# Three gate tiles of the merge fed into the chunk loop of the backward RWKV pass, and modulation blocks moved elsewhere

## The reference

```python
gates = jax.nn.sigmoid(h @ w_gate + b_gate)
acc = gates[..., :D_MODEL] * (ys[0] @ w_branch[0])
for i in range(1, N_BRANCH):
    acc = acc + gates[..., i * D_MODEL:(i + 1) * D_MODEL] * (ys[i] @ w_branch[i])
return acc @ w_o
```

## Time and profile before

| | us |
|---|---|
| median of 3 runs (lowest, highest) | 1781.99 (1780.87, 1786.96) |
| the profiled execution | 1783.33 |
| its span, first to last instruction | 1781.5 |
| PE busy | 1616.1 |
| DVE, ACT, POOL busy | 913.7, 783.3, 302.2 |
| granted PE clock, mean | 0.972 of full speed |

### The profile page before, as it was taken

The page is one execution under the profiler, slowest core; times in us unless marked ns, Lnnn a source line. Parts: engine busy times, 40 slices in busy tenths (PEclk is TensorE's granted clock), DMA queues, the critical chain, the costliest instruction groups (busy, mean ns, idle before and its releaser), DMA issues.

```text
span 1781.5 us, 35712 instructions
## 1 busy us (share of the span) xinstructions
PE 1616.1 (91%) x15480; PEld 1325.9 (74%) x15480; DVE 913.7 (51%) x1435; ACT 783.3 (44%) x1286; POOL 302.2 (17%) x241
## 2 busy tenths in 40 slices
PE   3799999977689999799999999899988789979997
PEld 1588767766566668488888886887876678979997
DVE  0444355466335433655555224655676436567754
ACT  1532355564225233634434323624765344565653
POOL 1023023512010000011112100131441110002210
PEclk9799999999899999899999999999999999989999
DMA  8742255504385212123222634734513275425554
GB/s 238 215 145 95 93 180 171 163 17 144 98 269 168 85 47 95 48 95 95 95 95 80 118 96 150 219 120 137 165 58 121 51 256 171 143 95 178 184 159 120
DMA packets 230347, 234.67 MB, mean 132 GB/s; under 512 B 5872, under 2 KB 217072, under 8 KB 230064
## 3 DMA queue, kind: packets, MB, share of 16 engines
q1 hardware_dynamic: 210560, 190.17, 34.0%
q0 software_dynamic: 15024, 35.92, 7.3%
q10 hardware_dynamic: 4608, 6.29, 1.1%
HBM read 216.63 MB, written 15.73 MB: 130 GB/s over the span
## 4 chain that ended last, share of the span: by engine, by line
PE 64%; DVE 5%; issue 5%; ACT 4%; DMA 1%; POOL 0%; ACTq 0%; DVEq 0%; POOLq 0%
PE ps L1792 15%; PE ps L1793 15%; PE ps L1794 15%; PE ps L2136 4%; PE ps L1994 2%; PE ps L1981 2%; PE ps L2033 1%; DVE wlo L1254 1%; PE ps L1830 1%; DVE X L1321 1%; ACT whi L849 1%; PE ps L1955 1%; PE ps L1815 1%; PE ps L1944 1%; DMA ring<-in_ffn_up 1%
## 5 line engine op out<-in xcount | busy, mean ns | idle before, releaser
L849 ACT ACTIVATE whi<-ring 128x1024 fp32r<-128x1024 f32 (+1 forms) x264 | 275.6, 1046 | 566.5 <-PE ps L1794 505.6
L1254 DVE TENSOR_TENSOR wlo<-ring,whi 128x1024 fp32r<-128x1024 f32 (+1 forms) x264 | 327.5, 1244 | 228.3 <-ACT whi L849 227.4
L1792 PE MATMUL ps<-H,whi 128*128 128x512 f32 (+1 forms) x656 | 220.8, 337 | 2.4 <-DVE wlo L1254 2.4
L1793 PE MATMUL ps<-H,whi 128*128 128x512 f32 (+1 forms) x656 | 220.6, 336 | 0.0
L1794 PE MATMUL ps<-H,wlo 128*128 128x512 f32 (+1 forms) x656 | 220.6, 336 | 0.0
L1792 PE MATMUL ps<-HR,whi 128*128 128x512 f32 (+1 forms) x592 | 211.6, 357 | 2.2 <-DVE wlo L1254 1.8
L1794 PE MATMUL ps<-HR,wlo 128*128 128x512 f32 (+1 forms) x592 | 207.7, 351 | 0.0
L1793 PE MATMUL ps<-HR,whi 128*128 128x512 f32 (+1 forms) x592 | 207.7, 351 | 0.0
L1792 PEld LDWEIGHTS ps<-H,whi 128*128 128x128 f32 x656 | 124.6, 190 | 16.0 <-issue 3.2
L1793 PEld LDWEIGHTS ps<-H,whi 128*128 128x128 f32 x656 | 124.6, 190 | 12.7
L1794 PEld LDWEIGHTS ps<-H,wlo 128*128 128x128 f32 x656 | 124.6, 190 | 12.7
(11 more groups left out here) (307 smaller groups left out, 3043.3 us busy)
## 6 DMA issues: line engine op xcount, KB each, us to landing
ring<-in_ada_w SPq DMA_DIRECT2D x48, 1024.0 KB, 5.8
ring<-in_ffn_up SPq DMA_DIRECT2D x44, 1024.0 KB, 5.1
ring<-in_w_gate SPq DMA_DIRECT2D x32, 1024.0 KB, 6.9
ring<-in_w_in SPq DMA_DIRECT2D x24, 1024.0 KB, 5.3
ring<-in_ffn_down SPq DMA_DIRECT2D x32, 512.0 KB, 3.8
WB<-in_w_branch POOLq DMA_DIRECT2D x8, 1024.0 KB, 7.9
ring<-in_w_o SPq DMA_DIRECT2D x8, 1024.0 KB, 5.2
ring<-in_ffn_down SPq DMA_DIRECT2D x16, 384.0 KB, 4.0
```

The costliest lines, as they stand in the source:

```text
L849: act.activation(whi[:, m % SPLIT, 0:kn, :], ring[:, SLOT[raw] % RING, 0:kn, P * half:P * half + P], ACT.Copy).then_inc(hi_done, 1)
L1254: dve.tensor_tensor(wlo[:, m % SPLIT, 0:kn, :], ring[:, SLOT[raw] % RING, 0:kn, P * half:P * half + P], whi[:, m % SPLIT, 0:kn, :].bitcast ...
L1792: pe.matmul(o[:, c0:c1], hi[:, i, :], part(0, k), start=(k == 0), stop=False)
L1793: pe.matmul(o[:, c0:c1], hi[:, i, :], part(1, k), start=False, stop=False)
```

## The change

The gate tiles (0, 2), (1, 2) and (0, 3), given as (tile, branch), are computed inside the chunk loop of the backward pass, a few matmuls at a time: 5 (layer 0) or 6 (layer 1) in each of its 14 gaps, the rest in the last. Their three splits move ahead of the loop. They use banks 5 to 7; the jobs of the backward loop share banks 0 to 4. The modulation blocks leave that loop: in layer 0 for the new point `mid` (three, between `ss` 1 and `ss` 2), with `end` of layer 0 keeping three; in layer 1 attention has seven points instead of three, the forward loop six instead of five, `mid` three. `mean` (with DVE's centring and ACT's squares) moves behind branch 2, `var` behind branch 0. `WB`'s first load goes out ahead of the wait for `y23`, and `state` moves from 112 to 168 KB to make room. The splits of `up` move from `wo` into ACT's squares of `X` and, on DVE, behind the residual. `gains` for `ffn_post` move to the end of the layer.

```diff
-READOUT = {(0, 2): "var", (0, 1): "g2"}
+READOUT = {(0, 2): "mean", (0, 0): "var", (0, 1): "g2"}
...
-CHUNK_FILL = {0: range(1, 7), 1: range(1, 6)}
+CHUNK_FILL = range(1, 7)
+GATES_AHEAD = [(0, 2), (1, 2), (0, 3)]
+GAP_PRODUCTS = {0: 5, 1: 6}
...
-        return [("chunk", l, d, c) for d in range(2) for c in CHUNK_FILL[l]]
+        return [("chunk", l, 0, c) for c in CHUNK_FILL]
...
-    before = [("att", 0, i) for i in range(0, 32, 2) if i % 8] + chunks(0)
-    after = [("end", 0, 0)] * 3 + [("att", 1, i) for i in range(0, 12, 4)] + chunks(1)
+    before = [("att", 0, i) for i in range(0, 32, 2) if i % 8] + chunks(0) + [("mid", 0, 0)] * 3 + [("end", 0, 0)] * 3
+    after = [("att", 1, i) for i in range(0, 14, 2)] + chunks(1) + [("mid", 1, 0)] * 3
...
+def chunk_gaps(l, d):
+
+    gaps, at = {}, 0
+    total = 3 * KT * len(GATES_AHEAD) if d else 0
+    order = [g for c in range(NCH) for g in (("cu", c), ("ch", c)) if g not in (("cu", 0), ("ch", NCH - 1))]
+    for n, g in enumerate(order):
+        more = total - at if n == len(order) - 1 else min(GAP_PRODUCTS[l], total - at)
+        gaps[g] = range(at, at + more)
+        at += more
+    return gaps
+
+
+def gates_done(l, d, gap):
+
+    return [("gate", l) + GATES_AHEAD[n // (3 * KT)] for n in chunk_gaps(l, d)[gap] if n % (3 * KT) == 3 * KT - 1]
 
...
+def in_first_group(name):
+
+    if name[0] in ("mean", "var", "g2"):
+        return True
+    return name[0] in ("br", "gate") and name[2] < 2 and name[2:] not in GATES_AHEAD and (name[0] == "gate" or name[3] != 3)
+
+
+def beside_gates(name, k):
+
+    if name[0] == "gate" and name[2:] in GATES_AHEAD:
+        return 5 + GATES_AHEAD.index(name[2:])
+    if name[0] in ("cu", "ch") and name[2] == 1:
+        return 4 if name[0] == "ch" else 2 * (name[3] % 2)
+    if name[0] in ("y1", "y23") and name[2] == 1:
+        return 2 * name[3]
+    return k
+
+
...
+        if g % NBANK == NBANK - 1 and in_first_group(name):
+            g += 1
+        k = beside_gates(name, g % NBANK)
...
-        state = at("state", 112, [NCH, 2, HD])
+        state = at("state", 168, [NCH, 2, HD])
...
+                    if J == 0:
+                        pool.wait_ge(mm_done, done_at(("y23", l, 1, 1)))
+                        for x in range(2):
+                            pool.wait_ge(gate_saved[x], 16 * 8 * (l + 1))
...
+                    if d == 1:
+                        act.wait_ge(kapw_done, 2 * it + 2)
+                        act.wait_ge(betaw_done, 2 * it + 2)
+                        split_until(half_no(("gate", l) + GATES_AHEAD[0]) + SPLIT)
                     for c in range(NCH):
...
+                            if (j, i) == GATES_AHEAD[0]:
+                                emptied(act, ("ch", l, 1, NCH - 2))
...
-                        split_until(min(half_no(("wo", l, j)) + 1 + SPLIT, half_no(("up", l, 0, 0)) + SPLIT))
+                        split_until(min(half_no(("wo", l, j)) + 1 + SPLIT, half_no(("up", l, 0, 0))))
...
-                split_until(half_no(("up", l, 0, 0)) + SPLIT)
                 norm_root(l, 1)
+                fill(("mid", l, 0))
                 for i in range(KT):
                     act.wait_ge(x_ready, 16 * l + i + 1)
                     square(SQB[:, i, c0:c1], X[:, i, c0:c1])
+                    if i >= 5:
+                        split_until(half_no(("up", l, 0, 0)) + i - 4)
...
+                    if d == 1:
+                        split_until(half_no(("gate", l) + GATES_AHEAD[0]) + SPLIT)
                     for p in range(2):
                         emptied(dve, ("tok", l, d, "b", p))
+                    dve.wait_ge(bonus_done, 4 * l + 2)
                     dve.memset(state[:, 0, :, :], 0.0).then_inc(state_zero, 1)
                     for p in range(2):
...
-                    if d == 1:
-                        split_until(half_no(("gate", l, 0, GATE_ORDER[0])) + SPLIT)
...
-                gains(l, (1, 2, 3))
+                fill(("mid", l, 0))
+                gains(l, (1, 2))
                 dve.wait_ge(x_back, 16 * (l + 1))
                 residual(l, 1, OB)
                 dve.wait_ge(x_ready, 16 * l + 8)
+                split_until(half_no(("up", l, 0, 0)) + SPLIT)
                 norm_apply(l, 2, X, YB, H2)
...
+            def gate_products(l, d, gap):
+
+                for n in chunk_gaps(l, d)[gap]:
+                    name = ("gate", l) + GATES_AHEAD[n // (3 * KT)]
+                    k, part = n % (3 * KT) // 3, n % 3
+                    c0, c1 = cols(l)
+                    if n % (3 * KT) == 0:
+                        if n == 0:
+                            pe.wait_ge(h_back[l], 32)
+                        ahead[name] = (job(name, JOB[name] - count[0]), next(halves(name)))
+                    o, (hi, lo) = ahead[name]
+                    last = pe.matmul(o[:, c0:c1], (hi, hi, lo)[part][:, k, :], HG[:, (0, 1, 0)[part], k, c0:c1],
+                                     start=(k == 0 and part == 0), stop=(k == KT - 1 and part == 2))
+                    if k == KT - 1 and part == 2:
+                        done(last)
+
+            ahead = {}
...
+                            gate_products(l, d, ("cu", c))
                             fill(("chunk", l, d, c), "mod")
...
+                            gate_products(l, d, ("ch", c))
                             fill(("chunk", l, d, c), "modt")
...
-                pe.wait_ge(h_back[l], 32)
                 for J in range(4):
                     for i in GATE_ORDER:
                         for j in (2 * J, 2 * J + 1) if i not in GATE_EARLY else ():
+                            if (j, i) in GATES_AHEAD:
+                                continue
...
+                        if READOUT.get((J, i)) == "mean":
+                            for p in range(2):
+                                emptied(pe, ("y23", l, 1, p))
+                                o = job(("mean", l, p))
...
                 sum_squares(l, 1, SQB)
+                fill(("mid", l, 0))
                 sum_squares(l, 2, SQB)
```

More of the change, by code:

```diff
@@ L778, in _ @@
                         .then_inc(h_back[l], 16)
-                pool.wait_ge(mm_done, done_at(("y23", l, 1, 1)))
-                for x in range(2):
-                    pool.wait_ge(gate_saved[x], 16 * 8 * (l + 1))
                 for J in range(4):
@@ L868, in norm_finish @@
                 no = 2 * l + k // 2
[L869 removed]
+                act.wait_ge(gains_ready, 3 * l + 1 + k // 2)
                 shift = 0 if k == 0 else 24
@@ L1156, in roots, with deviations @@
                            .then_inc(ln_root, 1)
-                for p in range(2):
-                    emptied(act, ("mean", l, p))
-                    act.activation(RO[:, p, c0:c1], YB[:, 6 + p, c0:c1], ACT.Square).then_inc(ln_sq, 1)
+                def deviations():
+                    for p in range(2):
+                        emptied(act, ("mean", l, p))
+                        act.activation(RO[:, p, c0:c1], YB[:, 6 + p, c0:c1], ACT.Square).then_inc(ln_sq, 1)
                 for J in range(4):
@@ L1268, in gains @@
             def gains(l, ks):
-                for n in range(24):
-                    if 0 not in ks or n < 8:
-                        emptied(dve, ("modt", l, n))
+                for n in {(0,): range(8), (1, 2): range(8, 20), (3,): range(20, 24)}[ks]:
+                    emptied(dve, ("modt", l, n))
                 for k in ks:
@@ L1688, in _ @@
                                 dve.tensor_tensor(o, o, gt, ALU.add).then_inc(gated, 1)
+                        if READOUT.get((J, i)) == "mean":
+                            centred()
                         if READOUT.get((J, i)) == "g2":
@@ L1738, in _ @@
                     emptied(dve, ("down", l, j))
+                gains(l, (3,))
                 residual(l, 3, F)
@@ L2112, in _ @@
                         done(last)
-                for p in range(2):
-                    emptied(pe, ("y23", l, 1, p))
-                    o = job(("mean", l, p))
-                    done(pe.matmul(o[:, c0:c1], K("heads"), YB[:, 6 + p, c0:c1], start=True, stop=True))
                 pe.wait_ge(ya_ready, 2 * l + 2)
@@ L2138, in _ @@
                             done(last)
-                        if READOUT.get((J, i)) == "var":
+                        if READOUT.get((J, i)) == "mean":
+                            for p in range(2):
+                                emptied(pe, ("y23", l, 1, p))
+                                o = job(("mean", l, p))
+                                done(pe.matmul(o[:, c0:c1], K("heads"), YB[:, 6 + p, c0:c1], start=True, stop=True))
+                        elif READOUT.get((J, i)) == "var":
                             for p in range(2):
```

30 lines of the change are left out of this document (14 added, 16 removed).

## The result

| | kernel before | kernel after |
|---|---|---|
| median, range of 4 runs each, us | 1784.47 (1780.87 to 1788.77) | 1806.45 (1803.06 to 1807.96) |
| profiled execution, time / span, us | 1783.33 / 1781.5 | 1806.97 / 1804.9 |
| granted TensorE clock over the span | 0.972 | 0.959 |

The ratio is 1.0121, 95% interval 1.0095 to 1.0147, that is 22 us. The prediction was 1798 (1782 to 1807), and its sum +16.1 us. In a later comparison the same kernel came out at 1.0121 again (1.0091 to 1.0150).

A forecast was written before the change was run, and what follows sets the result against it. TensorE, busy 91%, was taken as the bound, with short waits to win. Terms 0.1 + 0.8 + 4.4 + 5.8 + 4.5 + 0.5 = +16.1 us took 1783.33 to 1799.4, or 1798 on the median's scale; range 1782 to 1807.

The forecast's parts named there:

- the four places: In each layer: backward chunk loop, its tail up to the merge, norms between `wo` and `up`; second layer only: attention.
- Start of the loop: Start of the backward chunk loop: splits queued ahead delay the first `nu` product, losing 6.9 us per layer.
- The loop itself: Backward chunk loop: steps of 3.3 and 2.5 us plus slow clock lose 5.5 us (layer 0) and 1.1 (layer 1).
- To the `D` branch products: From the last `cu` to the first readout-dependent branch product: gains 12.3 us (layer 0) and 7.2 (layer 1).
- Norms: Between `wo` and `up`: late residual and splits among ACT's squares lose 4.4 us (layer 0) and 5.8 (layer 1).
- Attention and forward loop: Layer 1: four more modulation blocks in attention lose 4.5 us, one more in the forward loop 0.5.
- The feeding itself comes out even: Backward loop's start, loop and tail to the `D` branch products together: +0.1 us in layer 0, +0.8 in layer 1.
- the one in which more is late: Rival: loads competing ahead of the loop and banks holding up the merge cost 6 to 10 us more, 1806; 13%.
- The readout that keeps up: Rival: PE isn't stopped at the `D` branch products, 20 us more gained, kernel at 1778, not slower; 12%.

The follow-up runs named there:

- the early splits: Kernel after, with the fed gate tiles' three splits moved from the backward chunk loop's start into the last three levels of that pass: 1788.9 us, ratio 1.0021.
- the run with three products a gap: Kernel after plus four fixes (earlier splits, one activation table, readout earlier, additions later), three gate products a gap instead of five and six: 1762.3 us, 0.9889.
- The late additions: Kernel after, with DVE adding the `mid` blocks behind the residual and ACT copying each block's row behind a square of `X`: 1806.4 us, 1.0111.
- the two repairs: Kernel before, with one activation table for the readout's Ln and Exp and DVE's readout ahead of the second early branch's products: 1777.8 us, 0.9946.

## Why the prediction was right, and where it was off

The direction and the four places were right, and the time lies in the range, at its upper end (1806.45 of 1807); 16.1 us were forecast, 22 measured between the medians and 23.4 between the two spans that the terms below split.

1. *Start of the loop*, 6.9 us per layer: 6.5 and 6.4, by the queues described; confirmed by the early splits.
2. *The loop itself*, 5.5 and 1.1 us: 8.6 and 4.9. This is the term that was mis-sized, by 6.9 us in sum. The step was forecast as 3.3 and 2.5 us and is 3.71 and 2.81: the run with three products a gap shows 0.37 us a step that belong neither to the products nor to the recurrence, which I had not charged, over seven steps 2.6 us in each layer. The low clock costs 2.7 and 3.6 us instead of 2.0 and 1.1. Together that is a little more than what was missing. In the second execution of the same kernel layer 1 lost 3.1 us here instead of 4.9, so this term moves by some 2 us with the clock from one execution to the next.
3. *To the `D` branch products*, gain 12.3 and 7.2: from the last `cu` to there it is 33.2 and 22.6 us, a gain of 14.8 and 10.3. I had given the waits as about 6 and 11 us; they are 4.5 and 8.3. In layer 1 the first `GB` came sooner than the 6.4 us of the earlier trace rows: issued at 1475.8, used from 1480.1 on. In layer 0 ACT came to it only 6.4 us behind its issue and found it there. Of the 5.6 us more, 3.4 are lost again by the last branch product. A part of that is PE coming out of the wait slow: the eight products behind it take 5.9 us in layer 0, where they took 3.6 before; in layer 1 they take 3.8, but took 3.6 before too, behind a wait of 4.1, and there it is the gate products behind them that start 0.21 us apart at first, instead of 0.12.
4. *Norms*, 4.4 and 5.8 (the terms given for layer 0, 3.1 and 1.2, add up to 4.3): 4.4 and 5.5 over the whole path. The late additions show the order of DVE's list as the cause of the late residual.
5. *Attention and forward loop*, 4.5 and 0.5: 6.8 and 0.6. PE is at its limit in attention (68.5 of 72 us busy), a block costs 1.7 us, as much as its bare work and more, and none of it was hidden.

"The feeding itself comes out even" held to within 4 us (+2.6 and +2.1 against +0.1 and +0.8), partly by luck, since 6.9 us too little for the loop stand against 0.9 too much for the start and 2.2 too little for the gain behind it. And I had missed why so little is won. The kernel before already used its gaps: a step with a block took 2.53 us, an empty one takes 2.30 at the clock to which PE then falls, so a block of 1.5 us cost 0.2 there (0.7 against the 1.82 of an empty step at full clock, which doesn't last). In attention the same block costs 1.7. The change swapped one good filling for another and sent the first to places that charge for it in full (attention) or did so by the order of a list (the norms). Of the rivals, the one in which more is late has the measured number (1806), but by luck: what it gave as the cause, loads that compete ahead of the loop and banks that hold up the merge, isn't what the runs found. They found 7 us more in the loop. The readout that keeps up needed the two repairs to come true.

## What to carry to other kernels

Before work is fed into the gaps of a chain, count what fills them now, and where that goes. Put what must be ready for the feeding (here two splits on two engines) into an earlier idle time of those engines, not in front of the chain, since every engine takes its list in order and the wait is paid a second time in clock. An idle stretch takes a piece of work only if its inputs are there and if nothing that ends the stretch stands behind it in another engine's list.

## What the hardware showed that I had not expected

A loop whose gaps are empty falls from 1.00 to a granted clock of 0.50 within three steps, and one that starts at 0.50 stays there all the way, although PE is busy 10.8 of 14 us in it; with six 128x128 products in a step of 2.1 us it is 1.00 and PE is busy all of the time. So the bare step, 1.82 us at full clock, settles at 2.30, longer than the step with six products in it (2.09).

Ln and Exp in turn, each without a table that holds both, load a table each time, 1.28 us. Four such loads were 5.1 us of a chain of 10.

A step of the loop with products in its two gaps takes 0.37 us more than its matmuls cost elsewhere, in both layers, with PE busy all of the time and no wait in the records. That it is the change between 64x64 and 128x128 matmuls is argued, not shown.
